# Two-layer diffusion backbone on one core: where the first layer's weight tiles land, the order of its column groups, and who rounds what

## The reference, cut to what matters

```python
mod_lat = jnp.split((silu(c) @ ada_w[i] + ada_b[i])[:, None, :], 6, axis=-1)
h_lat = _rmsnorm(x_lat, norm1_g[i]) * (1 + mod_lat[1]) + mod_lat[0]
# layer 0
z = gelu(h @ w_in); u, v = z[..., :2048], z[..., 2048:]
v = rmsnorm(v, v_gain)                       # then chunked spatial mixing with w_s, b_s
y = (u * sv) @ w_out
x_lat = x_lat + mod_lat[2] * y
f = peer(rmsnorm(x_lat, norm2_g[i]) * (1 + mod_lat[4]) + mod_lat[3], w_q, k1, k2, u_tab, v_tab)
x_lat = x_lat + mod_lat[5] * f
```

## Time and profile before

| what | value |
|---|---|
| median of 3 runs | 1881.55 us (1880.54 to 1887.18) |
| the profiled execution | 1879.82 us, of which the span of its instructions is 1878.0 us |
| granted TensorE clock, mean | 0.996 of full speed |
| PE busy | 1842.4 us, 98% of the span |
| PEld, DVE, ACT, POOL busy | 1584.3, 1512.6, 956.8, 443.6 us |
| transfers | 376.33 MB, mean 200 GB/s |

### The profile page before, as it was taken

How to read it: one execution, slowest core, us unless ns; L and a number is a source line. 1 busy time by engine, 2 the same in 40 slices (tenths; PEclk the granted TensorE clock), 3 DMA queues, 4 the chain that set the end, 5 groups by cost and what they waited for, 6 DMA issues and landing times.

```text
span 1878.0 us, 35429 instructions
## 1 busy us (share of the span) xinstructions
PE 1842.4 (98%) x11760; PEld 1584.3 (84%) x11760; DVE 1512.6 (81%) x2815; ACT 956.8 (51%) x1592; POOL 443.6 (24%) x216
## 2 busy tenths in 40 slices
PE   7998999999999999999999999999999999999998
PEld 5798898888888888888888998888888888888887
DVE  6584689978998888888887588997999888885555
ACT  3643445655555544445555445565555544445444
POOL 4226478880000000000001158885000000000000
PEclk9999999999999999999999999999999999999999
DMA  7758455556655555578884445555655555555553
GB/s 292 283 211 301 143 173 187 182 186 208 220 180 168 173 175 175 171 270 327 318 292 162 141 163 185 181 188 192 221 202 168 170 177 175 171 173 191 195 190 134
DMA packets 104177, 376.33 MB, mean 200 GB/s; under 512 B 12464, under 2 KB 12464, under 8 KB 103856
## 3 DMA queue, kind: packets, MB, share of 16 engines
q1 hardware_dynamic: 103392, 373.37, 57.7%
q0 software_dynamic: 432, 2.10, 0.3%
q10 hardware_dynamic: 288, 0.06, 0.0%
HBM read 374.43 MB, written 1.05 MB: 200 GB/s over the span
## 4 chain that ended last, share of the span: by engine, by line
PE 85%; DVE 6%; DMA 5%; ACT 2%; issue 1%; POOL 1%; SPq 0%; ACTq 0%; DVEq 0%; POOLq 0%
PE ring L1722 19%; PE O L1777 13%; PE O L1779 12%; PE O L1778 12%; PE ring L1724 10%; DMA raw<-in_u 3%; PE ring L1694 3%; PE ring L1440 2%; PE ring L1441 2%; PE ring L1442 2%; DVE wL L853 2%; ACT wH L498 2%; PE ring L1715 2%; PE ring L1696 1%; PE O L1715 1%
## 5 line engine op out<-in xcount | busy, mean ns | idle before, releaser
L498 ACT ACTIVATE wH<-raw 128x1024 fp32r<-128x1024 f32 x606 | 642.5, 1061 | 819.1 <-DMA raw<-in_v 367.3
L1722 PE MATMUL ring<-hX,wH 128*128 128x512 f32 x1984 | 703.2, 398 | 0.0
L853 DVE TENSOR_TENSOR wL<-raw,wH 128x1024 fp32r<-128x1024 f32 x384 | 470.0, 1224 | 172.8 <-ACT wH L498 169.1
L1724 PE MATMUL ring<-hX,wL 128*128 128x256 f32 x1984 | 554.9, 280 | 0.0
L1722 PEld LDWEIGHTS ring<-hX,wH 128*128 128x128 f32 x1984 | 372.4, 188 | 85.8 <-issue 0.5
L1777 PE MATMUL O<-wH,gateH 128*128 128x512 f32 x1024 | 405.0, 396 | 0.0
L1779 PE MATMUL O<-wH,gateL 128*128 128x512 f32 x1024 | 399.5, 390 | 0.0
L1778 PE MATMUL O<-wL,gateH 128*128 128x512 f32 x1024 | 398.3, 389 | 0.0
L1724 PEld LDWEIGHTS ring<-hX,wL 128*128 128x128 f32 x1984 | 374.4, 189 | 0.0
L461 POOL TENSOR_TENSOR wL<-raw,wH 128x1024 fp32r<-128x1024 f32 x128 | 315.6, 2469 | 56.5 <-ACT wH L498 55.8
L1779 PEld LDWEIGHTS O<-wH,gateL 128*128 128x128 f32 x1024 | 192.2, 188 | 41.1
(11 more groups left out here) (213 smaller groups left out, 2408.0 us busy)
## 6 DMA issues: line engine op xcount, KB each, us to landing
raw<-in_u SPq DMA_DIRECT2D x256, 512.0 KB, 3.2
raw<-in_v SPq DMA_DIRECT2D x256, 512.0 KB, 3.2
ada_v<-in_ada SPq DMA_DIRECT2D x40, 512.0 KB, 4.5
raw<-in_w_in SPq DMA_DIRECT2D x32, 512.0 KB, 5.0
raw<-in_w_q SPq DMA_DIRECT2D x30, 512.0 KB, 3.2
ada_m<-in_ada SPq DMA_DIRECT2D x24, 512.0 KB, 5.8
ada_f<-in_ada SPq DMA_DIRECT2D x16, 512.0 KB, 7.2
raw<-in_w_out SPq DMA_DIRECT2D x16, 512.0 KB, 5.3
```

The source lines that it names most:

```text
L498: nc.scalar.activation(wH[s % RAW][:, :], (place or raw[s % RAW])[:, :], ACT.Copy).then_inc(s_h, 1)
L853: nc.vector.tensor_tensor(wL[s % RAW][:, :], raw[s % RAW][:, :], wH[s % RAW][:, :].bitcast(fp32), ALU.subtract).then_inc(s_low, 1)
L1722: mm(bank[:, :], wH[s][:, k * P:k * P + P], hX[:, k, :, :].rearrange("p two t -> p (two t)"), start=(k == 0), stop=False)
L1724: ins = mm(bank[:, 0:T], wL[s][:, k * P:k * P + P], hH[:, k, :], start=False, stop=(k == KT - 1))
```

## The change

It does six things.

1. Nine tiles of the front (w_v 3 to 11) get landing places of their own, `front_raw`, in memory that later holds the token values, the mixing weights and the keys. Their transfers wait for nothing. ACT now waits for `s_pe` itself before it writes the high part (`front_high`). Tiles 0 to 2 and 12 to 15 use `raw`.
2. Four of the 24 later ada tiles are loaded right behind w_v tiles 12 to 15, without a wait, and summed on DVE between the low parts of these tiles; `OUT_ADA` sums 12 instead of 16 in w_out. In w_out the ada transfers follow tiles 5 to 12 instead of 3 to 14. The first w_u tile is issued ahead of the small loads.
3. For s > 0, PE takes both halves of column group 0 first, then both of group 1, then both of group 2.
4. The gain and the shift of a chunk are made on ACT (`front_h`: two 1-column activations), h gets the gain alone on DVE, and the shift enters when ACT rounds and when DVE makes the low part. The inverse root is spread into `O[1]`; DVE scales chunks 0, 1 by it at k = 0, 1 and the other six at k = 2.
5. POOL makes the low parts of w_out tiles 0 to 2 in four instructions of 256 columns each (`low_early`).
6. In ACT's order, the rounding of w_u tile 3 comes ahead of the last squares and the root, and the rounding of `p_in` tile 2 at the end of layer 0 comes behind the copies to `otok`.

```diff
--- before.py
+++ after.py
...
             ada_f = [sb(f"ada_f{x}", [P, D], at=ad) for x in range(16)]
+        front_raw = []
+        for under, count in ((64, 4), (88, 2), (100, 3)):
+            with ExitStack() as fr:
+                sb(f"under_front{under}", [P, under * T], at=fr)
+                front_raw += [sb(f"front_raw{under}_{x}", [P, D], at=fr) for x in range(count)]
         with ExitStack() as ad:
...
         s_first_l = sem("s_first_l")
+        s_unit = sem("s_unit")
+        s_fraw = [sem(f"s_fraw{x}") for x in range(9)]
+        s_gain = sem("s_gain")
+        s_rooted = sem("s_rooted")
         s_xn = sem("s_xn")
...
         ADA_SLOTS = tuple(s for s in range(12) if s % 3 < 2)
-        OUT_ADA = (1, 1, 1, 1, 2, 1, 2, 1, 1, 1, 1, 1, 1, 1, 0, 0)
+        OUT_ADA = (1,) * 12 + (0,) * 4
         BLOCK_GROUPS = 3
+        FRONT_RAW = range(3, 12)
+        def raw_count(t):
+            skipped = sum(x % RAW == t % RAW for x in FRONT_RAW)
+            return 16 * (t // RAW + 1) - (16 * skipped if t >= FRONT_RAW.stop else 0)
         BLOCK_TILES = 4 * BLOCK_GROUPS
...
-            def load_ada(place, m):
-                sp.wait_ge(s_acc, m - len(place) + 1)
+            def load_ada(place, m, first=False):
+                if not first:
+                    sp.wait_ge(s_acc, m - len(place) + 1)
                 sp.dma_start(place[m % len(place)][:, :], ada_d[m]).then_inc(s_ada[m % 4], 16)
...
-                load(stream_dram["w_v", 0], 0, t // 4, t % 4, first=(t < 4))
+                if t in FRONT_RAW:
+                    sp.dma_start(front_raw[t - 3][:, :], stream_dram["w_v", 0][t]).then_inc(s_fraw[t - 3], 16)
+                else:
+                    if t >= RAW:
+                        sp.wait_ge(s_pe, t - RAW + 1)
+                    sp.dma_start(raw[t % RAW][:, :], stream_dram["w_v", 0][t]).then_inc(s_raw[t % RAW], 16)
...
                 if g == 0:
-                    load(stream_dram["w_v", 0], 0, 0, 0, first=True)
+                    load_gate(0)
                 load_front(4 * g)
                 load_front(4 * g + 1)
-                if g == 0:
-                    load(stream_dram["w_v", 0], 0, 0, 1, first=True)
-                else:
-                    load_gate(3 * g)
-                    load_gate(3 * g + 1)
+                load_gate(3 * g + (g == 0))
                 load_front(4 * g + 2)
                 load_front(4 * g + 3)
+                if g:
+                    load_gate(3 * g + 1)
                 load_gate(3 * g + 2)
+            m = ADA_FRONT
             for t in range(BLOCK_TILES, 16):
                 load_gate(t)
+                load_ada(ada_m, m, first=True)
+                m += 1
+            load(stream_dram["w_u", 0], W_U, 0, 0)
             for dst, src in small_loads:
                 sp.dma_start(dst, src).then_inc(s_small, 16)
-            m = ADA_FRONT
             for t in range(16):
-                load(stream_dram["w_u", 0], W_U, t // 4, t % 4)
+                if t:
+                    load(stream_dram["w_u", 0], W_U, t // 4, t % 4)
                 if t < 8 or t > 11:
...
                 load(stream_dram["w_out", 0], W_OUT, t // 4, t % 4)
-                if 2 < t < 15:
+                if 4 < t < 13:
                     load_ada(ada_m, m)
...
                         sp.wait_ge(s_pooled, PG)
-                    sp.wait_ge(s_raw[0], 4 * base + 16)
+                    sp.wait_ge(s_raw[0], raw_count(base))
                     sp.dma_start(spare[:, :], src[4]).then_inc(s_raw[0], 16)
...
+            def low_early(s, n=1):
+                pool.wait_ge(s_h, W_OUT + s + 1)
+                for at in range(0, D, 2 * P):
+                    ins = nc.gpsimd.tensor_tensor(wL[s][:, at:at + 2 * P], raw[s][:, at:at + 2 * P],
+                                                  wH[s][:, at:at + 2 * P].bitcast(fp32), ALU.subtract)
+                ins.then_inc(s_l1, n)
             def low_out(i, s, n=1):
...
                 for at in (0, HALF):
-                    nc.gpsimd.tensor_tensor(wL[t % RAW][:, at:at + HALF], raw[t % RAW][:, at:at + HALF],
+                    src = front_raw[t - 3] if t in FRONT_RAW else raw[t % RAW]
+                    nc.gpsimd.tensor_tensor(wL[t % RAW][:, at:at + HALF], src[:, at:at + HALF],
                                             wH[t % RAW][:, at:at + HALF].bitcast(fp32), ALU.subtract).then_inc(s_first_l, 1)
...
                         front_low(t)
-                    low_out(0, 0, W_OUT + 1)
-                    for s in range(1, 4):
-                        low_out(0, s)
+                    low_early(0, W_OUT + 1)
+                    low_early(1)
+                    low_early(2)
+                    low_out(0, 3)
                     with pool.Fori(1, 4) as i:
...
-                act.wait_ge(s_raw[s % RAW], 16 * i + (base + s) // 4 * 16 + 16)
+                act.wait_ge(s_raw[s % RAW], 16 * i + raw_count(base + s))
                 nc.scalar.activation(wH[s % RAW][:, :], (place or raw[s % RAW])[:, :], ACT.Copy).then_inc(s_h, 1)
...
-                act.wait_ge(s_xn, k + 1)
-                nc.scalar.activation(hH[:, k, :], sq[:, k, :], ACT.Copy).then_inc(s_hH, 1)
+                act.wait_ge(s_acc, 2 * k + 1)
+                nc.scalar.activation(gs[:, 0, k:k + 1], modcol(0, 1, k, 1), ACT.Identity, scale=n1[:, k:k + 1],
+                                     bias=adab[:, KT + k:KT + k + 1]).then_inc(s_gain, 1)
+                act.wait_ge(s_acc, 2 * k + 2)
+                nc.scalar.activation(modcol(0, 0, k, 1), modcol(0, 0, k, 1), ACT.Identity,
+                                     bias=adab[:, k:k + 1]).then_inc(s_gain, 1)
+                act.wait_ge(s_gain, 2 * k + 2)
+                high_h(0, k)
+            def front_high(t):
+                if t in FRONT_RAW:
+                    act.wait_ge(s_fraw[t - 3], 16)
+                    if t >= RAW:
+                        act.wait_ge(s_pe, t - RAW + 1)
+                    nc.scalar.activation(wH[t % RAW][:, :], front_raw[t - 3][:, :], ACT.Copy).then_inc(s_h, 1)
+                else:
+                    split_high(W_V, 0, t)
+            act.wait_ge(s_unit, 1)
             for g in range(4):
...
                 if g:
-                    split_high(W_V, 0, 3 * g)
-                split_high(W_V, 0, 3 * g + 1)
+                    front_high(3 * g)
+                front_high(3 * g + 1)
                 front_h(2 * g + 1)
-                split_high(W_V, 0, 3 * g + 2)
+                front_high(3 * g + 2)
                 if g == 2:
...
-                    split_high(W_V, 3, 0)
+                    front_high(12)
+                    front_high(13)
                     tokens_out(0)
-                    split_high(W_V, 3, 1)
+                    front_high(14)
                     tokens_out(1)
-                    split_high(W_V, 3, 2)
+                    front_high(15)
                     tokens_out(2)
-                    split_high(W_V, 3, 3)
                     for g in range(3):
...
                     for t in range(16):
+                        ahead(W_U, t // 4, t % 4)
                         if t == 0:
...
                                 .then_inc(s_vstd, 1)
-                        ahead(W_U, t // 4, t % 4)
                         act.wait_ge(s_pe, W_U + t + 1)
...
                 if layer < LAYERS - 1:
-                    for s in (1, 2, 3):
+                    for s in (1, 2):
                         ahead(base, 31, s)
...
                 nc.scalar.activation(otok[:, 1, 512:1024], O[3][:, :], ACT.Copy).then_inc(s_oc_a, 1)
+                if layer < LAYERS - 1:
+                    ahead(base, 31, 3)
                 for j in range(KT):
...
                                         wH[s % RAW][:, 0:width].bitcast(fp32), ALU.subtract).then_inc(s_l0, n)
-            def front_rest(k):
-                dve.wait_ge(s_hH, k + 1)
-                nc.vector.tensor_tensor(hL[:, k, :], sq[:, k, :], hH[:, k, :].bitcast(fp32), ALU.subtract).then_inc(s_hin, 1)
...
             dve.wait_ge(s_bias, BIAS)
-            after(step(nc.vector.tensor_scalar(adab[:, KT:2 * KT], adab[:, KT:2 * KT], 1.0, None, ALU.add)))
+            nc.vector.scalar_tensor_tensor(adab[:, KT:2 * KT], adab[:, KT:2 * KT], 1.0, n1[:, 0:KT], ALU.add, ALU.mult)\
+                .then_inc(s_unit, 1)
             dve.wait_ge(s_cond, 2)
+            def rooted(k):
+                return step(nc.vector.tensor_tensor(sq[:, k, :], XT[:, k, :], O[1][:, 0:T], ALU.mult))
             for k in range(KT):
...
                     inverse_root(0)
+                elif k == 2:
+                    for j in range(2, KT):
+                        last = rooted(j)
+                    nc.vector.memset(tick[:, 0:1], 0.0).then_inc(s_rooted, 1)
+                    low_h(0, 1)
                 else:
-                    front_rest(k - 1)
-                dve.wait_ge(s_acc, 2 * k + 1)
```

(32 more changed lines are left out.)

## The result

The kernel after takes 1863.63 us (median of 5 runs, 1861.84 to 1868.03) against 1881.55 of the kernel before (1880.18 to 1887.18): the ratio is 0.9903, 95% interval 0.9882 to 0.9924, so 17.9 us faster. The two traces therefore differ by 13.8 us of span (1878.0 to 1864.2) where the medians differ by 17.9.

A forecast was written before the change was run, and what follows sets the result against it. PE was busy 98% of the span, so only its gaps and clock could gain. Front 10.4, group 3 0, w_u 1.0, w_out 7.5 and layer end 2.5 sum to 21.4 us: 1858.4 profiled, median 1860, range 1853 to 1871.

The forecast's parts named there:

- three signs of being wrong: DVE's h or low part waiting 1 us per chunk; clock under 1 from 20 to 40 us; late w_u tiles.
- Front: Start to group 3: landing places, block order and roundings on ACT gain 10.4 us, bounds 4 and 13.
- The start: Front's first block: fewer DVE rescalings, gain and shift on ACT, so PE starts 2.3 us earlier, bounds 0 and 2.9.
- Waiting at s = 0: Front, chunks 0 and 1: PE still waits 3.4 us, for low parts of chunk 1 and tile 1.
- the 0.9 of chunks 2 to 7: Front: with DVE at 4.0 us a chunk, 0.9 us of waiting stays in all.
- Rival 1: Front: DVE becomes the bound through the port, 5.8 us a chunk; gain 3.5 instead of 10.4, 1867 us; chance 0.12.
- The passage into w_u: Group 3 into w_u: PE's time covers four more ada tiles; 0 us, bounds 0.4 gained and 2 lost.
- w_u, 1.0 forecast: w_u: tile 3 rounded ahead of the last squares and root removes a 1.01 us wait; 1.0 gained, bounds 0 and 1.0.
- w_out, 7.5 forecast: w_out: earlier tiles 4 and 5, less waiting and slow clock; 10.8 - 3.3 = 7.5 us gained, bounds 3 and 10.8.
- rival 2: w_out: wait only moves from tile 4 to 6, 4 to 5 us, clock falls; gain 2, 1866 us; chance 0.12.
- Layer end: End of layer 0: PE's 2.75 us idle for copies goes as a rounding moves behind them; 2.5 gained, bounds 1.0 and 2.7.
- Rivals 3 and 4: Front: transfers arrive out of issue order, 1879 us, chance 0.08; PE's clock drops early, slower, 1899 us, chance 0.04.

The follow-up runs named there:

- three mended together: Kernel after with small loads moved, chunk 1's low part first, and the layer-end p_in low part made inside the norm: 1858.94 us, ratio 0.9871.

## Why the prediction was right, and where it was not

**Direction and size.** 1860 was forecast and 1863.63 measured, inside 1853 to 1871. The named mechanisms held: tiles that have a place no longer hold up the queue, and w_out's gap closes. But of its three signs of being wrong the prediction met one in full, a clock under 1 between 20 and 40 us (0.69 and 0.88 above), and a second for another reason: w_u's tiles are late, behind the small loads. And w_out begins 4.1 us earlier where 11.5 was said.

**Front, 10.4 forecast, 8.4 measured.** The start gave 1.7 of 2.3; it differs by execution, from 15.15 to 16.58 in the profiles of the other kernels with this start. The prediction called all of the 12.4 us above 24 x 1.38 waiting; PE's waits in before are 8.2 of it, the rest are blocks that take longer around a wait. After, 5.7 stay (38.88 less 33.2) where 4.3 was forecast. Waiting at s = 0 is 3.57 us (0.64, 0.33, 2.60), for which 3.4 was left, and its largest piece is the one named: the low part of chunk 1 behind six rescalings. DVE in order of time, kernel after:

```profile
18.52 1.27 DVE L1033 TENSOR_SCALAR sq<-sq,gs 128x256 f32<-128x256 f32 x1
...
20.85 2.07 DVE L1012 TENSOR_TENSOR sq<-XT,O 128x256 f32<-128x256 f32 x6
22.84 1.34 DVE L955 SCALAR_TENSOR_TENSOR hX<-sq,mod,hX 128x256 fp32r<-128x256 f32 x1
...
25.25 0.34 DVE L1033 TENSOR_SCALAR sq<-sq,gs 128x256 f32<-128x256 f32 x1
...
28.48 1.43 DVE L1033 TENSOR_SCALAR sq<-sq,gs 128x256 f32<-128x256 f32 x1 [0.21 <-ACT gs L588]
```

For chunks 2 to 7, 0.9 of waiting was left. Here there is none, but the two blocks behind the 2.60 take 1.93 and 2.42 us instead of 1.37, at half clock: 1.6 us that no term had. This may not be simply a loss on top. With the layer end undone, the clock stays at 1.00 behind the same 2.60; the waits of 0.85 and 0.86 shown for it appear in its place, and group 3 comes 40.5 us after the first block, not 38.9. With the quarters undone it is the same, 39.4. It reads as if a PE that is slow early lets its feed get ahead; no run sets the clock by itself, so this is not shown. The term that was too small is the 0.9 of chunks 2 to 7: 1.6 us of slow clock stand in its place here, and waits of 1.05 (0.16 and 0.89) and 1.88 us (0.17, 0.85 and 0.86) in those two. Why the two at full clock lose more than the one that was slow is not settled.

POOL is what is nearest to its limit. POOL in order of time, kernel after:

```profile
27.23 24.30 POOL L488 TENSOR_TENSOR wL<-front_raw,wH 128x512 fp32r<-128x512 f32 x18 [3.32 <-ACT wH L602]
```

Eighteen halves back to back, 1.35 each, make 8.1 per s against PE's 8.2: "it just fits" held to the tenth.

**Rival 1, DVE as the bound.** Its mechanism is there, its condition is not. h with one scalar takes 0.34 us alone (25.25) and 1.27 or 1.43 beside a POOL half. That is what the Trainium skill ("SBUF — State Buffer", "Who interferes with whom") says of the port that DVE and GpSimd share, and the rows agree for this form. They agree for the form with two scalars too, which the prediction took to be free of it from the earlier trace rows: without part 4 it takes 1.33 us at 30.58, beside a half. In before all eight took 0.41, and POOL was at work beside none of them. Only every second h meets a half in this way, and chunks come every 3.6 to 4.0 us (25.25, then 32.51 and 40.43 two chunks each), faster than PE's 4.1. The kernel without part 4 shows DVE as the bound: 4.96 us a chunk (the rival said 5.8), DVE never idle.

**The passage into w_u, 0 forecast, bounds 0.4 gained and 2 lost; measured, a wait of 3.71 at w_u tile 1 and a slow clock behind it.** This is the step that failed. (In the table the loss falls into the stage that ends as w_out begins, since the wait comes behind w_u's first tile.) It counted the four ada tiles against PE's time for group 3, but not what the first w_u tile's move leaves behind it. SP in order of time, kernel after:

```profile
57.92 0.33 SPq L348 DMA_DIRECT2D raw<-in_w_in  x1
...
60.66 0.43 SPq L394 DMA_DIRECT2D ws<-in_ws  x1
61.14 0.43 SPq L354 DMA_DIRECT2D ada_m<-in_ada  x1
61.61 0.43 SPq L348 DMA_DIRECT2D raw<-in_w_in  x1
```

and ACT's rounding of that second tile:

```profile
70.17 1.06 ACT L532 ACTIVATE wH<-raw 128x1024 fp32r<-128x1024 f32 x1 [5.31 <-DMA raw<-in_w_in]
```

Tile 0 is issued at 57.92, tile 1 only 3.7 us later, behind `bs`, `ws` (512 KB each), four loads of 4 to 8 KB and an ada tile, and it lands 8.5 us after its issue instead of 4.4. The engines carried 196 GB/s from 60 to 62, while the small loads went through, and 410 again from 64 on. Moving the small loads removes the wait, as the experiment shows. Its length differs from profile to profile: 1.91, 2.10, 1.37, 1.66, 1.68 and 1.60 us in the six other kernels with places and the same order of these transfers. So the 3.71 is the longest of seven, which would account for most of the 2.3 us by which the profiled execution lies above its median; the other executions have no trace, so this is not shown.

**w_u, 1.0 forecast, 4.9 lost.** The wait of 1.01 ahead of tile 3 is gone in the kernel after, as forecast, but another lies hidden behind the longer one at tile 1: in five profiles with shorter waits at tile 1, 0.42 to 0.45 and 0.2 stand at tiles 3 and 4. The loss is the 3.71, about 1.5 of slow clock behind it (3.37 x 0.33 and 4.00 x 0.09) and the 0.62 ahead of w_out's first tile, less the 1.01.

**w_out, 7.5 forecast, 8.7 measured.** The 7.21, the 1.55 and about 2 us of slow clock are gone (10.8), and 0.32, 0.37 and 1.69 have come. The 1.69 is the wait ahead of tile 6 that was named, at 1.0; rival 2, 4 to 5 us there and a clock that falls, did not occur. With the ada tiles two tiles earlier it occurs at tile 4, at 4.03. Tiles behind 6 did not wait at all (1.3 had been left), and the quarters left less than the 1.0.

**Layer end, 2.5 forecast, 2.3 measured, but not from the edit alone.** The 2.75 us are gone. The wait of 1.39 is new: POOL waits for the moved rounding (982.07 to 983.13), issues three transfers, and makes its three low parts just when DVE makes its own, so that one holds up the other. DVE and POOL in order of time, kernel after:

```profile
985.18 4.29 DVE L889 TENSOR_TENSOR wL<-raw,wH 128x512 fp32r<-128x512 f32 x1
...
985.21 3.72 POOL L467 TENSOR_TENSOR wL<-raw,wH 128x512 fp32r<-128x512 f32 x3
```

In before this DVE instruction took 1.50 us. The remainder is clock: in before it fell to 0.61 from 996 to 1000, behind the 2.75, and transposes and squares took 7.0 us (996.03 to 1003.05); with the edit undone the same wait (2.68) is followed by 1.00, and they take 5.4 (980.13 to 985.51). The prediction didn't count this clock, nor the new wait.

**Rivals 3 and 4.** Neither DVE nor ACT waited for a transfer between 16 and 47 us, so the front's transfers came in time, and the clock's falls cost single microseconds, not thirty.

## What to carry to other kernels

Give a transfer that has to come early a place that waits for nothing, and then look at who feeds the next step: here the places were worth 4.1 us at group 3 and the roundings another 4.2, and without the places the roundings and the order brought nothing there. When a load is moved ahead in a strict queue, price the one that comes after it too, with every small load that now stands between the two. And a wait that is mended shows the next one: of three mended together only the one from SP's queue showed a gain.

## What was not expected of the hardware

The granted clock does not answer to the length of a wait alone. Behind PE's wait of 2.60 us in the front it was 0.69 in the kernel after and 0.57 to 0.64 behind 2.58 to 2.61 in five others, but 1.00 with the quarters or the layer end undone, behind 2.61 and 2.60; behind 2.21 it was 0.63 with the places alone and 1.00 behind 2.20 without part 4. What decides is not settled by these runs. One fall of this kind is worth 1.6 us of PE's time in the front. The two kernels that had none there waited 1.05 and 1.88 us more later, and group 3 did not come earlier in them.
